# A ring of eight places instead of nine, a second gate slab held on chip, and TensorE one row behind VectorE

## What is computed

```python
h = h + token_mixer(rms_norm(h, norm_mix_g[i]), ...)
h = h + peer_ffn(rms_norm(h, norm_ffn_g[i]), ...)
h = h + per_layer_embedding(h, p[i], w_ple[i], ple_norm_g[i], w_ple_gate[i])
...
u = expert_u[ids]                                   # 8 heads x 16 experts a token
pre = jnp.einsum('chkd,cd->chk', u, xc)
act = gate * jax.nn.gelu(pre, approximate=False)
return jnp.einsum('chk,chkd->cd', act, expert_v[ids])
...
gate = jax.nn.sigmoid((rms_norm(h, ple_norm_g) @ w_ple_gate))
```

## Time and profile before

| | us |
|---|---|
| median of 3 executions | 1501.56 |
| the profiled execution, its own time | 1501.45 |
| span of the profile (first to last instruction) | 1499.6 |
| TensorE busy | 1114.0 (74%) |
| VectorE busy | 1051.0 (70%) |
| ScalarE busy | 575.0 (38%) |
| GpSimd busy | 580.2 (39%) |
| HBM read / written | 597.17 MB / 1.05 MB |

### The profile page before, as it was taken

How to read it: one execution, slowest core, us unless ns; L and a number is a source line. 1 busy time by engine, 2 the same in 40 slices (tenths; PEclk the granted TensorE clock), 3 DMA queues, 4 the chain that set the end, 5 groups by cost and what they waited for, 6 DMA issues and landing times.

```text
span 1499.6 us, 18452 instructions
## 1 busy us (share of the span) xinstructions
PE 1114.0 (74%) x6408; PEld 439.9 (29%) x6408; DVE 1051.0 (70%) x2698; ACT 575.0 (38%) x1803; POOL 580.2 (39%) x516
## 2 busy tenths in 40 slices
PE   9996676996687566896668878797566877666666
PEld 7672232451124322351112434343011211111112
DVE  3799987678957376779995457686798664444446
ACT  0335456243432166333333246533234433333332
POOL 0045444454323234346442245355344343434330
PEclk9999787997789777996668988898567976666778
DMA  9469999999999999999999999999999999999993
GB/s 369 184 277 422 421 420 421 420 411 420 420 406 405 415 420 420 422 420 421 421 420 379 417 421 420 420 414 418 419 421 420 410 422 421 422 420 421 421 422 123
DMA packets 88204, 599.42 MB, mean 400 GB/s; under 512 B 9776, under 2 KB 10288, under 8 KB 22576
## 3 DMA queue, kind: packets, MB, share of 16 engines
q0 software_dynamic: 73728, 536.90, 86.4%
q1 hardware_dynamic: 14224, 61.09, 10.2%
q10 hardware_dynamic: 160, 0.26, 0.1%
HBM read 597.17 MB, written 1.05 MB: 399 GB/s over the span
## 4 chain that ended last, share of the span: by engine, by line
DMA 40%; PE 28%; DVE 20%; ACT 5%; issue 4%; POOL 2%; SPq 0%; POOLq 0%; DVEq 0%; ACTq 0%
DMA ring<-in_rows,ids 38%; PE acc L661 10%; DVE ring L1505 9%; PE bank L829 3%; PE bank L1043 3%; PE bank L1130 2%; DMA ring<-in_w_in 2%; PE bank L697 2%; POOL ring L626 2%; PE bank L702 1%; ACT diag L1222 1%; PE acc L697 1%; ACT act_w L1219 1%; DVE wb L1899 1%; PE bank L700 1%
## 5 line engine op out<-in xcount | busy, mean ns | idle before, releaser
L626 POOL DMA_INDIRECT ring<-in_rows,ids x512 | 580.0, 1133 | 879.8 <-PE acc L661 646.1
L661 PE MATMUL acc<-ring,diag 64*64 64x512 f32 x3968 | 665.8, 780 | 302.0 <-ACT diag L1222 300.1
L1505 DVE CUSTOM_DVE_ANT_0 ring<-ring,xc 128x1024 f32<-128x1024 f32 x504 | 609.7, 1225 | 340.3 <-DMA ring<-in_rows,ids 336.5
L1213 ACT ACTIVATE gel<-pre 128x1 f32<-128x1 f32 x512 | 103.2, 202 | 765.4 <-DVE pre L1505 753.6
L661 PEld LDWEIGHTS acc<-ring,diag 64*64 64x64 f32 x3968 | 138.9, 159 | 772.1 <-ACT diag L1222 669.8
L1222 ACT ACTIVATE diag<-cst,act_w 128x64 f32<-128x64 f32 x512 | 178.2, 348 | 16.7
L1219 ACT ACTIVATE act_w<-gate,gel 128x1 f32<-128x1 f32 x512 | 150.9, 295 | 16.6
L697 PE MATMUL bank<-hT,ring 128*128 128x128 f32 x384 | 50.2, 286 | 21.4 <-DMA ring<-in_w_in 18.4
L829 PE MATMUL bank<-held,hT 128*128 128x512 f32 x128 | 59.0, 602 | 1.3 <-DVE hT L1547 1.3
L697 PEld LDWEIGHTS bank<-hT,ring 128*128 128x128 f32 x384 | 46.8, 197 | 37.7 <-issue 32.6
L1043 PE MATMUL bank<-hT,held 128*128 128x128 f32 x384 | 46.1, 278 | 2.6 <-DVE hT L1544 2.6
(11 more groups left out here) (294 smaller groups left out, 1021.9 us busy)
## 6 DMA issues: line engine op xcount, KB each, us to landing
ring<-in_w_in SPq DMA_DIRECT2D x24, 978.0 KB, 10.9
held<-in_w_out SPq DMA_DIRECT2D x8, 1024.0 KB, 24.9
held<-in_w_query SPq DMA_DIRECT2D x8, 1024.0 KB, 24.6
ring<-in_rows,ids POOLq DMA_INDIRECT x512, 16.2
ring<-in_w_gate SPq DMA_DIRECT2D x6, 1024.0 KB, 11.8
held<-in_w_gate SPq DMA_DIRECT2D x5, 1024.0 KB, 24.5
held<-in_w_ple SPq DMA_DIRECT2D x2, 1024.0 KB, 31.0
held_latent<-in_w_latent SPq DMA_DIRECT2D x2, 768.0 KB, 28.0
```

The costliest lines, as they stand in the source:

```text
L626: pool.indirect_dma_start(out=ring[:, at % RING, :], out_offset=None, in_=rows, in_offset=bass.IndirectOffsetOnAxis(ap=index, axis=0),).th ...
L661: last = pe.matmul(acc[rows_of(c), r, :], diag[rows_of(r), j, :], ring[rows_of(r), j, D:][:, cols_of(c)], start=False, stop=True, skip_gro ...
L1213: act.activation(gel[:, j:j + 1], pre[:, j:j + 1], ACT.Gelu).then_inc(gelued, 1)
L1505: dve.tensor_tensor_reduce(out=u, in0=u, in1=x, scale=1.0, scalar=0.0, op0=ALU.mult, op1=ALU.add, accum_out=pre[:, j:j + 1]).then_inc(dott ...
```

## The change

The ring has eight places instead of nine, and `held` has one slab more, so the room is the same (8 KB a partition). Slab 1 of layer 0's `w_gate` is loaded once at the beginning, behind slab 0 in SyncE's queue, and passes through the ring neither in window 1 nor in window 2: four gate slabs go through the ring instead of six. `behind` of TensorE is 1 instead of 2, in its own walk and in `ring_order`. VectorE's and ScalarE's are what they were.

```diff
@@ -44,9 +44,9 @@
-RING = 9
+RING = 8
 WSLOT = 2048
-GATE_HELD = 1
+GATE_HELD = 2
 HELD = KT + GATE_HELD
@@ -167,7 +167,7 @@
 def ring_order():
     entries = []
-    rows = Stream(lambda step, k: entries.append(("row", step, k)), 2, EARLY)
+    rows = Stream(lambda step, k: entries.append(("row", step, k)), 1, EARLY)
@@ -1198,7 +1198,7 @@
-            walk(Stream(experts, 2, EARLY), {"front": front, "leave": leave, "rest": rest, "choose": choose, "sort": sort, "embed": embed, "lift": lift,
+            walk(Stream(experts, 1, EARLY), {"front": front, "leave": leave, "rest": rest, "choose": choose, "sort": sort, "embed": embed, "lift": lift,
```

## The result

The change made the kernel slower: 1514.47 us (median of 4 executions, 1513.67 to 1516.16) against 1501.85 us of the kernel before on the same chip. The ratio is 1.0082, interval 1.0069 to 1.0094, so 12.3 us (10.4 to 14.1). The forecast was 1499.5 us and its range ended at 1505.5 us.

What follows compares the result with a forecast made beforehand. The prediction took the kernel to be bound by DMA bytes. Its terms, -5.0 (slabs), 0 (held slab), 0 (row 8), +1.0 (thin spots) and +2.0 (SyncE's wait), gave -2.0 us: 1499.5 us, range 1495.5 to 1505.5 us.

Steps and rivals of the forecast that it cites:

- Bytes bound the kernel: Whole kernel: DMA engines are the bound as long as something is queued; compute matters only where it frees places too late.
- Two slabs: Streamed part: two gate slabs fewer through the ring, 2 x 2.49 us of DMA time, gain 5.0 us.
- Row 8: Step 0 start: row 8's gather must wait until row 0 is used, no unused ninth place; 0 us, at most 1.5.
- the held slab's 0 us: Beginning: one more held slab loads while the DMA engines idle from 60 to 80 us; cost 0, without that cover 2.5.
- Ring and lag "together": Shorter ring and TensorE one row behind cancel where rows lie ready; at thin spots they cost 1.0 us, bounds 0 to 7.2.
- thin spots: Stretches around 300, 640 and 995 us where the queue before the DMA is shortest: gathers land after 9.1 or 8.0 us.
- SyncE's new wait: Window 1: w_in slab 7 waits until slab 4 is used, query slabs queue behind; DMA gap 2.0 us, bounds 0 and 3.
- The dip: Window 2: rate falls to 182, then 370 GB/s, 5 us each; counted as costing nothing, since rows arrive every 2.5 us.
- Rival (a): Window 2's rate dip is real, so freeing a place earlier in the gate stage gains: 1495.1 us, chance 0.33 including 1496.5 us.
- Rival (b): End of `choose`: VectorE takes over the bound, so the slabs save only 2.5 us, total 1502 us; chance 0.22.
- Rival (c): Hops: ring runs dry as TensorE waits for a diagonal before dense work; 1505.7 us, 1510.7 at worst; chance 0.17.
- a new stop of VectorE on rows: Hops around 300, 640 and 995 us: the sign that would show the prediction wrong as a whole.

## Why the prediction was wrong

The change was forecast at -2.0 us and came out at +12.3, 14.3 us further. 10.3 us of these came back when TensorE and the ring's order were two rows behind in the hops alone. The other 4.0 are left with eight places and the better lag (+2.0 against -2.0).

**Bytes bound the kernel: right.** The window with rows alone is as long as before, and most of what window 2 lost shows as missing bytes (11.1 of 13.1 us).

**Two slabs, -5.0 us: right.** Measured alone -5.3 us (-7.2 to -3.3); with eight places the second held slab gave 6.3. The Trainium skill ("DMA: Bandwidth & Descriptors", Specifications) gives some 358 GB/s for HBM; by it the estimate was 5.9 us, and the interval holds both. The rate of 421 GB/s in the trace stands against that figure as a limit for this core.

**Row 8, 0 us (to 1.5): left open.** With eight places alone, the first forget gates, L1680, are at 120.62 us, against 120.60 before, so the dense work is not late. But row 8's gather goes out at 105.75 us instead of 103.65, and from 100 to 120 us the rate is 379 GB/s instead of 416, which is 1.8 us of bytes (with nine places and one behind it is 421). No run prices this by itself; window 0 of that kernel ends 3.8 us later, with more bytes missing around 230 and 310 us. In the change L1680 is at 122.68 us because of the lag (123.44 us with the lag alone), which the prediction did not look at there; repairing that gained nothing that could be measured. Against the held slab's 0 us nothing speaks.

**Ring and lag "together", +1.0 us (0 to 7.2): this is the step that failed.** Alone they cost 10.4 and 8.3 us. The prediction said that "these two cancel" where rows lie ready. That is true in the slab stages (366 and 364 GB/s with the ring alone, 419 and 420 with both). It named the exception, a row that still waits for ScalarE, where "the wait moves in front of TensorE's dense work", and then sized it by the landing times of the gathers, one arrival at most. But that wait has nothing to do with arrivals. Its length is ScalarE's dense block of 7.0 us, and it delays `sums`, then VectorE, then the next rows. Everything for that figure was in the trace of before: `sums` started at 891.76 us with the next row's diagonal still to come, and that row's L661 could start only at 895.49 us. One row put before `sums` meant an estimated 895.5 + 1.1 - 891.8 = 4.8 us, and the prediction did not look there. The two edits that keep `sums` from waiting for that diagonal, one by TensorE's lag and one by ScalarE's, gave back 10.3 and 6.6 us. The prediction had 1.0 for the two, and 3.0 with what else hangs on the missing place (row 8 and SyncE's wait). Measured, all of that cost 12.3 + 5.3 = 17.6 us.

**The margins.** The sum took thin spots as they stood in the trace of before, as if a stretch stayed the same when its order changes. It also put the ring's price at thin spots in the hops alone; the ring of eight with two behind lost most in the slab stages (366 and 364 GB/s), which had shown 412 and 420 GB/s before and didn't look thin. Part of that ring's price is SyncE's new wait, which it has too: 364 GB/s instead of 415 from 500 to 520 us, 2.4 us of bytes.

**SyncE's new wait, +2.0 us: the mechanism was right, its worth wrong.** The query slabs went out behind the use of slab 4, at 515.59 us, and 2.7 us of bytes are missing between 510 and 520 us; the prediction had 1.8 and a place at 508 to 512 us. But closing the gap with one query slab changed the time by 0.1 us by the ratio and 0.6 us by the medians. The intervals are wide enough for 2 us either way, but the traces show where it went: a later thin spot took it back. The term should have been near 0 in a kernel that runs dry later anyway.

**The dip, counted as nothing: not settled.** Rival (a) as a forecast, 1495.1 us, falls with the total. In the kernel with nine places and hops two behind the two windows of the earlier trace rows show 394 and 397 GB/s instead of 182 and 370, 2.8 us of bytes, and it is no faster than before. But it lacks bytes elsewhere that the kernel before had: over the whole stretch from 800 to 880 us the rate is 404 against 400 GB/s, 0.8 us, and window 2 is 3.1 us longer (362.6 against 359.5). In the change the same stretch has 413 GB/s, 2.5 us more bytes than before, and loses them in the hops. So no run closes the dip and leaves the rest alone.

**Rival (b)** falls. The kernel that leaves slab 1 out would have gained 2.5 us by it and gained 5.3 (3.3 to 7.2), and its rate between 680 and 780 us, where VectorE is busiest, stays at 419 to 423 GB/s: the DMA engines have no gap there. **Rival (c)** is what happened: TensorE waits for a diagonal before its dense work, the places come free later. It had a chance of 0.17 and 1510.7 us at the worst; the result lies beyond that, for the reason above. Its sign was to be "a new stop of VectorE on rows" in the hops, and this is not what the trace shows. The waits between 880 and 1004 us before, and between 880 and 1016 us after (waited for, us in total, times, longest):

```profile
DVE ring L1505 <- DMA ring<-in_rows,ids: 16.8, 16, 2.2
...
DVE F L1680 <- PE bank L792: 0.9, 1, 0.9
```

```profile
DVE ring L1505 <- DMA ring<-in_rows,ids: 8.9, 8, 1.6
...
DVE F L1680 <- PE bank L792: 5.5, 1, 5.5
```

VectorE waits for rows less than before, 8 times and not 16, for it now waits for TensorE and rows lie ready meanwhile. So DMA engines that have gone idle for want of places need not show as a longer wait for rows.

What stays open is how the 6.8 us of the missing place are spread, and how much of them a better order of the slabs would give back; that wasn't tried. Why the ring alone costs 10.4 us, when rows landed after 16.2 us in the median, is located in its trace (the slab stages, the start, SyncE's wait) but was not taken apart by runs.

## What to carry to other kernels

When engines work in order and one is moved nearer to the engine that feeds it, look at every block of dense work between two rows: what was due behind the block may now be due before it, and the price is up to the whole block of the feeding engine (here a wait of 6.39 us on a block of 7.0), not the time of one row. In a kernel that is bound by a queue of transfers, price each edit alone and then the pair: a smaller lag gave back what the lost place took in one stage and cost more than that in another (8.2 us as a whole). And sum up the gains at thin spots with care: a stretch that is repaired in front of another thin one can give nothing.

## What the hardware showed beyond that

A load that SyncE issued behind 4.7 MB of its own, with rows going on in GpSimd's queue, took from 516.67 to 545.75 us, 29 us for 1 MB, where in the change, with nothing of SyncE's in front, the same slab went out at 515.22 us and landed after 4.7 us. Rows went on in GpSimd's queue in both. So for that slab the place in its own queue mattered more than the rows in the other.

The mean rate of the DMA engines fell to 182 GB/s for 5 us in the kernel before, and the dot products at 819.49 and 821.97 us, right behind it, still found their rows 2.5 us apart. How much such a dip costs, if anything, these runs do not show.
